# One 2048-column split instruction per weight chunk and engine in place of two of 1024 columns

## The chip, the cores and the metric

The kernel runs on one core of a Trainium2 chip. The metric is the device time of one execution in microseconds (us), taken as the median of several runs. A profiled execution of the same program gives the trace; times inside it count from the start of its span.

## The reference

One inference step of a two-layer decoder trunk, all in float32: 256 prompt tokens and 64 sample tokens (320 together), model width 1024. Each layer adds a token mixer to the residual and then a channel mixer, both after an RMS norm. The mixer is one wide projection, a chunked spatial gate, a gated linear recurrence, two branch projections and an output projection. The channel mixer is a dense SwiGLU in layer 0, and in layer 1 a top-2-of-8 mixture of SwiGLU experts, cut to

```python
h = h + mix
hn = rms_norm(h, norm_ffn_g[l])
# layer 0
h = h + (silu(hn @ w_gate) * (hn @ w_up)) @ w_down
# layer 1
for e in range(8):
    h = h + combine[..., e:e+1] * swiglu(hn, w_gate[e], w_up[e], w_down[e])
```

The weights are most of the data: eight experts of three 1024 x 2816 matrices each.

## The kernel before, in words

Each product of float32 matrices is made from three matmuls in a faster format: a weight w is split into a high part (w rounded) and a low part (w minus the high part), the moving data likewise, and high x high, high x low and low x high are summed in PSUM.

All weights stream through one ring in the order in which they are used. The unit is a chunk of 2048 columns on 128 partitions (1 MB). A chunk is made of two pieces of 1024 columns; `RING` is six pieces, so three chunks (`AHEAD` is 3). There are three rings of the same shape: `raw` (float32 from HBM), `whi` (high) and `wlo` (low). For piece p these steps follow each other:

- SyncE (the SP queue) waits until `low_done` counts p - 6 + 1, then loads the piece into its slot of `raw` (L495 in the dense layers, L503 in the experts).
- ScalarE (ACT) waits for the load and, through `pe_mark`, until TensorE (PE) has used piece p - 6, then copies `raw` to `whi` (`split_high` at L638, `high_of` at L850), and counts `high_done`.
- VectorE (DVE) waits for `high_done` and writes `raw` minus `whi` to `wlo` (`split_low` at L920, `low_of` at L1273), and counts `low_done`.
- PE waits for `low_done` and multiplies: L1413 to L1415 (dense), L1429 to L1431 (products by rows of tokens), L1694 to L1696 (expert down), L1703 to L1705 (expert gate and up).

ACT and DVE run one list each, chunk by chunk. In the entry of chunk c they split the two pieces of chunk c + 3. Between these two splits stands the work that empties the tiles of chunk c out of PSUM: activations of gates and of q, u, v on ACT (L664, L864), products, residual additions and squares (L954, L649, L931, L1287). Behind the second split stands the rest of the entry: the recurrence, the layer norm of v, the scores, and in the experts the turning of hidden rows. Because an engine works its list in order, a split that waits for PE holds back what is written after it.

In the dense layers a chunk is 48 matmuls of 320 columns. Between stages stand the RMS norms: PE is done with the last chunk, DVE adds the residual, ACT squares, DVE sums, PE reduces over partitions (L1438), ACT takes the root (L655), PE spreads it (L1446), and the next products follow.

An expert is 33 chunks of 12 matmuls of 512 columns (or 24 of 256): 11 of gate, 11 of up in turn, then 11 of down. PE takes the routed tokens of the next expert together (`gather`, L1657) after the last up chunk, number 21, and adds an expert's result back three chunks into the next expert (`scatter`, L1734). DVE then adds the six parts to the sum (`add_sums`, L1316), in its list between the splits of chunks 5 and 6 of that next expert; PE's gate products of the second group wait for the first of these additions.

Of the kernel before, what the change touches and what calls it, by code (L numbers as in the profile page):

```python
# [5 lines left out]
def hybrid_trunk_program(nc, A, OUT):  # L6
# [15 lines left out]
    F = mybir.dt.float32  # L22
# [599 lines left out]
    def _(act):  # L622
# [8 lines left out]

        def split_high(c, half):
            n = piece_width(c)
            p = 2 * c + half
            act.wait_ge(raw_full[p % RING], 16 * (p // RING + 1))
            if p >= RING:
                act.wait_ge(pe_mark, mark_after[p - RING])
            fn(whi[:, p % RING, 0:n], raw[:, p % RING, 0:n], ACT.Copy).then_inc(high_done, 1)  # L638

# [28 lines left out]
        for j in range(KD):  # L668
            square(0, j)
        split_high(0, 0)  # L670
        split_high(0, 1)
        norm(0)
        for c in range(1, AHEAD):
            split_high(c, 0)
            split_high(c, 1)

# [5 lines left out]
        for L in range(LAYERS):  # L682
            if L:
                norm(2 * L)
            for i, (sec, part) in enumerate(MIX):
                c = base(L) + i
                split_high(c + AHEAD, 0)
                if SAMPLE_AT < i <= SAMPLE_AT + H:
# [49 lines left out]
                if sec == "w_out":  # L738
                    for j in (2 * part, 2 * part + 1):
                        square(2 * L + 1, j)  # L740
                split_high(c + AHEAD, 1)
                if i == GATES_AT:
# [48 lines left out]
            if L % 2 == 0:  # L791
                norm(2 * L + 1)

                act.wait_ge(pstate_out, 16 * (L + 1))
                act.wait_ge(vrow_out, 16 * (L + 1))
                for q in s0_out:
                    act.wait_ge(q, 16 * (L + 1))
                for i, (sec, part) in enumerate(FFN):
                    c = first_chunk[(L, "gate")] + i
                    split_high(c + AHEAD, 0)  # L800
                    if sec == "gate":
                        if part:
                            act.wait_ge(dve_emptied, tile[(L, "up", 2 * part - 1)][3])
                        for j in (0, 1):
                            empties(L, sec, 2 * part + j, sg[:, j, :], ACT.Silu)
                    if sec == "down" and part % 3 == 2:
                        for j in (0, 1):
                            square(2 * L + 2, 2 * (part // 3) + j)
                    split_high(c + AHEAD, 1)
# [34 lines left out]

        def high_of(item, i, half):
            n = piece_width(NDENSE + i % NEC)
            p = 2 * i + half
            act.wait_ge(raw_full[p % RING], 16 * (2 * NEC // RING) * item + 16 * (2 * NDENSE // RING + p // RING + 1))
            act.wait_ge(pe_mark, 2 * NEC * item + (MB + p - RING + 1))
            fn(whi[:, p % RING, 0:n], raw[:, p % RING, 0:n], ACT.Copy).then_inc(high_done, 1)  # L850

        def chunk(item, i, last, ahead):

            if i + AHEAD < last:
                high_of(item, i + AHEAD, 0)
            if i >= NEC:
# [3 lines left out]
            if kind == "gate" and closed:  # L860
# [3 lines left out]
                fn(sge[:, j % 2, 0:cols], bank[2 * (j % 2)][:, 0:cols], ACT.Silu).then_inc(gate_emptied, 1)  # L864
            if i + AHEAD < last:
                high_of(item, i + AHEAD, 1)
            if kind == "up" and closed:
# [16 lines left out]
        def extra(item, n):  # L884
            for i in range(AHEAD):
                for half in range(2):
                    high_of(item, i, half)
            expert_in_high(item)
            for i in range(NEC):
                chunk(item, i, NEC, False)  # L890
# [15 lines left out]
    def _(dve):  # L906
# [8 lines left out]

        def split_low(c, half):
            n = piece_width(c)
            p = 2 * c + half
            dve.wait_ge(high_done, p + 1)
            v.tensor_tensor(wlo[:, p % RING, 0:n], raw[:, p % RING, 0:n],  # L920
                            whi[:, p % RING, 0:n].bitcast(F), ALU.subtract).then_inc(low_done, 1)

# [41 lines left out]
        add_square(0, KD - 1)  # L964
        split_low(0, 0)
        split_low(0, 1)
        dve.wait_ge(prm_ready, 1)

        v.tensor_tensor(lbt[:, 0], prm[:, P_LB + H:P_LB + 2 * H], prm[:, P_LB:P_LB + H], ALU.subtract).then_inc(lb_ready, 1)
        norm(0)  # L970
        for c in range(1, AHEAD):
            split_low(c, 0)
            split_low(c, 1)
        dve.wait_ge(lb_exp, 1)
# [6 lines left out]
        for L in range(LAYERS):  # L981
# [12 lines left out]
            for i, (sec, part) in enumerate(MIX):  # L994
                c = base(L) + i
                split_low(c + AHEAD, 0)
                if sec == "branch_a":
# [89 lines left out]
                split_low(c + AHEAD, 1)  # L1087
                if i == 0:
# [100 lines left out]
            if L % 2 == 0:  # L1189
                norm(2 * L + 1)  # L1190
                for i, (sec, part) in enumerate(FFN):
                    c = first_chunk[(L, "gate")] + i
                    split_low(c + AHEAD, 0)
                    if sec == "up":
# [11 lines left out]
                    split_low(c + AHEAD, 1)  # L1206
                    if sec == "up":
# [60 lines left out]

        def low_of(item, i, half):
            n = piece_width(NDENSE + i % NEC)  # L1270
            p = 2 * i + half
            dve.wait_ge(high_done, 2 * NEC * item + (2 * NDENSE + p + 1))
            v.tensor_tensor(wlo[:, p % RING, 0:n], raw[:, p % RING, 0:n],  # L1273
                            whi[:, p % RING, 0:n].bitcast(F), ALU.subtract).then_inc(low_done, 1)

        def chunk(item, i, last, ahead, e=None):

            if i + AHEAD < last:
                low_of(item, i + AHEAD, 0)
            if i >= NEC:  # L1280
# [3 lines left out]
            if kind == "up" and closed:  # L1284
# [3 lines left out]
                                ALU.mult).then_inc(he_ready, 1)  # L1288
            if i + AHEAD < last:
                low_of(item, i + AHEAD, 1)  # L1290
            if kind == "up" and closed:
# [57 lines left out]
        with dve.If(any_extra(dve)):  # L1349

            with dve.Fori(1, BLOCKS) as b:
                dve.wait_ge(pick_ready, NE)
                dve.wait_ge(shift_done, b)
                v.tensor_scalar(slot[:], slot[:], -float(CAP), None, ALU.add).then_inc(shift_done, 1)
                with dve.Fori(0, NE) as e:
                    more, item = extra_block(dve, b * NE + e - NE)
                    with dve.If(more):
                        choose(item, e, b + 1)
                        for i in range(AHEAD):
                            for half in range(2):  # L1360
                                low_of(item, i, half)
# [419 lines left out]
```

## Time and profile before

| | us |
|---|---|
| median of 3 runs | 1717.65 (1717.3 to 1717.74) |
| span of the profiled execution | 1711.7 |
| PE busy in it | 1651.6 |
| DVE busy | 1218.1 |
| ACT busy | 992.3 |

The span is the time from the first to the last instruction of the profiled execution; the median of the runs lies 5.95 us above it. Busy time is the sum over the whole span. The experts take the stretch from 860 to 1690 us; the dense stages lie before it. A chain of work, as the page gives it, is followed back from the last instruction to what released each step; a wait is the idle time of an engine, put down to what ended it.

### The profile page before, as it was taken

Reading aid. Unit: us, or ns where it says so; the run is one execution under the profiler, and the core shown is the slowest. Engines: PE = TensorE matmul, PEld = TensorE weight load, DVE = VectorE, ACT = ScalarE, POOL = GpSimd, SP = SyncE. Lnnn points to the kernel's source line nnn. Section 1 sums busy time; section 2 is a strip of 40 time slices with the busy share of each in tenths; the row PEclk is TensorE's granted clock in tenths of the full one; section 3 lists DMA queues with packets and bytes.
Section 4 is the critical chain, followed back from the end, with each engine's and each line's share of the span. In section 5 each row is a group of like instructions: output and inputs, shape, how many; then the busy total and the mean of one; then the engine's idle time right before and its main releaser. Section 6 shows DMA issues by size and latency. Waiting matters only on the chain.

```text
span 1711.7 us, 26087 instructions
## 1 busy us (share of the span) xinstructions
PE 1651.6 (96%) x9174; PEld 1450.4 (85%) x9175; DVE 1218.1 (71%) x1521; ACT 992.3 (58%) x1179; POOL 70.9 (4%) x87
## 2 busy tenths in 40 slices
PE   6989999999998989999899999999999999999996
PEld 5889999999998879999788888888888888888884
DVE  6677347544445487437478997979979799797996
ACT  5663234444334754224376786767867677776783
POOL 3020110000000020110000000000000000000000
PEclk9999999999998999989899999999999999999998
DMA  7434445355444334444278998989989899898994
GB/s 218 136 102 134 137 141 144 115 149 151 140 151 123 111 111 127 142 136 124 62 261 306 336 377 291 347 290 340 379 289 347 291 340 376 294 347 289 342 365 152
DMA packets 219374, 385.73 MB, mean 225 GB/s; under 512 B 11936, under 2 KB 103120, under 8 KB 219296
## 3 DMA queue, kind: packets, MB, share of 16 engines
q1 hardware_dynamic: 215920, 372.84, 63.8%
q0 software_dynamic: 3376, 11.83, 2.5%
q8 instruction: 51, 0.84, 0.2%
q14 instruction: 27, 0.22, 0.0%
HBM read 378.33 MB, written 6.29 MB: 225 GB/s over the span
## 4 chain that ended last, share of the span: by engine, by line
PE 90%; DVE 4%; ACT 4%; issue 2%; DMA 0%; SPq 0%; DVEq 0%; ACTq 0%
PE bank L1413 11%; PE bank L1415 10%; PE bank L1414 10%; PE bank L1703 9%; PE bank L1705 9%; PE bank L1704 9%; PE bank L1694 5%; PE bank L1695 5%; PE bank L1696 5%; PE bank L1657 4%; PE bank L1538 2%; ACT weights_high L638 1%; PE bank L1668 1%; PE bank L1588 1%; PE bank L1583 1%
## 5 line engine op out<-in xcount | busy, mean ns | idle before, releaser
L1273 DVE TENSOR_TENSOR weights_low<-weights_raw,weights_high 128x1024 fp32r<-128x1024 f32 x522 | 624.6, 1221 | 60.7 <-ACT weights_high L850 54.2
L850 ACT ACTIVATE weights_high<-weights_raw 128x1024 fp32r<-128x1024 f32 x522 | 548.6, 1061 | 158.9 <-PE bank L1705 63.5
L920 DVE TENSOR_TENSOR weights_low<-weights_raw,weights_high 128x1024 fp32r<-128x1024 f32 (+1 forms) x186 | 225.3, 1216 | 299.9 <-ACT weights_high L638 299.8
L638 ACT ACTIVATE weights_high<-weights_raw 128x1024 fp32r<-128x1024 f32 (+1 forms) x186 | 193.5, 1045 | 250.6 <-PE bank L1415 241.1
L1413 PE MATMUL bank<-moving_high,weights_high 128*128 128x320 f32 x992 | 318.2, 321 | 6.3 <-DVE moving_low L944 5.3
L1414 PE MATMUL bank<-moving_low,weights_high 128*128 128x320 f32 x992 | 313.5, 316 | 0.0
L1415 PE MATMUL bank<-moving_high,weights_low 128*128 128x320 f32 x992 | 313.2, 316 | 0.0
L1703 PE MATMUL bank<-weights_high,expert_in_high 128*128 128x512 f32 (+1 forms) x768 | 289.2, 377 | 0.0
L1705 PE MATMUL bank<-weights_high,expert_in_low 128*128 128x512 f32 (+1 forms) x768 | 286.2, 373 | 0.0
L1704 PE MATMUL bank<-weights_low,expert_in_high 128*128 128x512 f32 (+1 forms) x768 | 286.0, 372 | 0.0
L1413 PEld LDWEIGHTS bank<-moving_high,weights_high 128*128 128x128 f32 x992 | 192.7, 194 | 11.9 <-issue 8.3
L1414 PEld LDWEIGHTS bank<-moving_low,weights_high 128*128 128x128 f32 x992 | 192.9, 194 | 0.0
L1415 PEld LDWEIGHTS bank<-moving_high,weights_low 128*128 128x128 f32 x992 | 192.5, 194 | 0.0
L1705 PEld LDWEIGHTS bank<-weights_high,expert_in_low 128*128 128x128 f32 x768 | 145.0, 189 | 25.6
L1703 PEld LDWEIGHTS bank<-weights_high,expert_in_high 128*128 128x128 f32 x768 | 145.2, 189 | 25.0 <-issue 0.2
L1704 PEld LDWEIGHTS bank<-weights_low,expert_in_high 128*128 128x128 f32 x768 | 145.3, 189 | 24.4
L1694 PE MATMUL bank<-weights_high,expert_hidden_high 128*128 128x512 f32 x352 | 140.3, 398 | 0.0
L1695 PE MATMUL bank<-weights_low,expert_hidden_high 128*128 128x512 f32 x352 | 139.5, 396 | 0.0
L1696 PE MATMUL bank<-weights_high,expert_hidden_low 128*128 128x512 f32 x352 | 139.5, 396 | 0.0
L1696 PEld LDWEIGHTS bank<-weights_high,expert_hidden_low 128*128 128x128 f32 x352 | 66.3, 188 | 16.1
L1694 PEld LDWEIGHTS bank<-weights_high,expert_hidden_high 128*128 128x128 f32 x352 | 66.3, 188 | 15.8
L1695 PEld LDWEIGHTS bank<-weights_low,expert_hidden_high 128*128 128x128 f32 x352 | 66.3, 188 | 15.8
(283 smaller groups left out, 1880.3 us busy)
## 6 DMA issues: line engine op xcount, KB each, us to landing
weights_raw<-in_moe_w_gate SPq DMA_DIRECT2D x176, 512.0 KB, 5.5
weights_raw<-in_moe_w_up SPq DMA_DIRECT2D x176, 512.0 KB, 5.4
weights_raw<-in_moe_w_down SPq DMA_DIRECT2D x176, 512.0 KB, 5.2
weights_raw<-in_w_in SPq DMA_DIRECT2D x80, 512.0 KB, 3.5
weights_raw<-in_dense_w_gate SPq DMA_DIRECT2D x22, 512.0 KB, 3.8
weights_raw<-in_dense_w_up SPq DMA_DIRECT2D x22, 512.0 KB, 3.8
weights_raw<-in_w_out SPq DMA_DIRECT2D x16, 512.0 KB, 3.4
weights_raw<-in_dense_w_down SPq DMA_DIRECT2D x16, 512.0 KB, 3.4
```

The lines of the kernel that those rows point to most:

```text
L850: fn(whi[:, p % RING, 0:n], raw[:, p % RING, 0:n], ACT.Copy).then_inc(high_done, 1)
L920: v.tensor_tensor(wlo[:, p % RING, 0:n], raw[:, p % RING, 0:n], whi[:, p % RING, 0:n].bitcast(F), ALU.subtract).then_inc(low_done, 1)
L1273: v.tensor_tensor(wlo[:, p % RING, 0:n], raw[:, p % RING, 0:n], whi[:, p % RING, 0:n].bitcast(F), ALU.subtract).then_inc(low_done, 1)
L1413: mm(b[:, 0:T], whi[:, p % RING, w], mh[:, k0 + k, :], start=first and k == 0, stop=False)
L1414: mm(b[:, 0:T], whi[:, p % RING, w], ml[:, k0 + k, :], start=False, stop=False)
L1415: ins = mm(b[:, 0:T], wlo[:, p % RING, w], mh[:, k0 + k, :], start=False, stop=last and ends)
L1694: mm(bank[down_bank(ahead) + hh][:], heh[:, kk, :], whi[:, p % RING, w], start=kk == 0, stop=False)
L1695: mm(bank[down_bank(ahead) + hh][:], heh[:, kk, :], wlo[:, p % RING, w], start=False, stop=False)
L1696: ins = mm(bank[down_bank(ahead) + hh][:], hel[:, kk, :], whi[:, p % RING, w], start=False, stop=kk == KF - 1)
L1703: mm(b[:, 0:cols], xeh[:, kk, :], whi[:, p % RING, w], start=kk == 0, stop=False)
L1704: mm(b[:, 0:cols], xeh[:, kk, :], wlo[:, p % RING, w], start=False, stop=False)
L1705: ins = mm(b[:, 0:cols], xel[:, kk, :], whi[:, p % RING, w], start=False, stop=kk == KD - 1)
```

## The change

Each engine splits a chunk with one instruction over both pieces of the ring (2 x 1024 columns side by side) where it had one for each piece. ACT waits for both loads and until PE has used both pieces of the old chunk; `high_done` and `low_done` then rise by two at once. DVE waits until both pieces are high. The split takes the place of the first of the two old splits in each engine's list; the second one is gone. The loads, the ring and PE's list are as before, so a load still waits for the same count of `low_done`.

```diff
-        def split_high(c, half):
+        def split_high(c):
             n = piece_width(c)
-            p = 2 * c + half
-            act.wait_ge(raw_full[p % RING], 16 * (p // RING + 1))
+            p = 2 * c
+            s = p % RING
+            act.wait_ge(raw_full[s], 16 * (p // RING + 1))
+            act.wait_ge(raw_full[s + 1], 16 * (p // RING + 1))
             if p >= RING:
-                act.wait_ge(pe_mark, mark_after[p - RING])
-            fn(whi[:, p % RING, 0:n], raw[:, p % RING, 0:n], ACT.Copy).then_inc(high_done, 1)
+                act.wait_ge(pe_mark, mark_after[p + 1 - RING])
+            fn(whi[:, s:s + 2, 0:n], raw[:, s:s + 2, 0:n], ACT.Copy).then_inc(high_done, 2)
...
-                split_high(c + AHEAD, 0)
+                split_high(c + AHEAD)
...
-                split_high(c + AHEAD, 1)
...
-        def high_of(item, i, half):
+        def high_of(item, i):
...
-            act.wait_ge(pe_mark, 2 * NEC * item + (MB + p - RING + 1))
-            fn(whi[:, p % RING, 0:n], raw[:, p % RING, 0:n], ACT.Copy).then_inc(high_done, 1)
+            act.wait_ge(raw_full[s], landed)
+            act.wait_ge(raw_full[s + 1], landed)
+            act.wait_ge(pe_mark, 2 * NEC * item + (MB + p - RING + 2))
+            fn(whi[:, s:s + 2, 0:n], raw[:, s:s + 2, 0:n], ACT.Copy).then_inc(high_done, 2)
...
-        def split_low(c, half):
+        def split_low(c):
             n = piece_width(c)
-            p = 2 * c + half
-            dve.wait_ge(high_done, p + 1)
-            v.tensor_tensor(wlo[:, p % RING, 0:n], raw[:, p % RING, 0:n],
-                            whi[:, p % RING, 0:n].bitcast(F), ALU.subtract).then_inc(low_done, 1)
+            p = 2 * c
+            s = p % RING
+            dve.wait_ge(high_done, p + 2)
+            v.tensor_tensor(wlo[:, s:s + 2, 0:n], raw[:, s:s + 2, 0:n],
+                            whi[:, s:s + 2, 0:n].bitcast(F), ALU.subtract).then_inc(low_done, 2)
...
-            if i + AHEAD < last:
-                low_of(item, i + AHEAD, 1)
```

`low_of` in the experts changes as `split_low` does, and the calls in the channel mixer and in the rarely taken extra blocks likewise.

## Rows read from the trace of the kernel before

**Rows 1.** The page: busy time by engine, and the ending chain by engine.

```profile
PE 1651.6 (96%) x9174; PEld 1450.4 (85%) x9175; DVE 1218.1 (71%) x1521; ACT 992.3 (58%) x1179; POOL 70.9 (4%) x87
...
PE 90%; DVE 4%; ACT 4%; issue 2%; DMA 0%; SPq 0%; DVEq 0%; ACTq 0%
```

**Rows 2.** The ending chain in order of time: start, us, what; two gathers, transposes.

```profile
1029.26 8.26 PE bank L1657 x48
1093.78 0.59 PE bank L1668 x4
1134.58 8.26 PE bank L1657 x48
```

**Rows 3.** Busy time by engine in one expert's period, clock, DMA share, GB/s.

```profile
1150.70:1256.00 105.30, 105.30 (x506) 86.71 (x506) 91.93 (x94) 76.97 (x84) 0.00 (x0) 1.00 0.91 329
```

**Rows 4.** Waits of PE's weight loads, 860 to 1690 us: total, times, longest.

```profile
PEld bank L1711 <- issue: 1.3, 8, 0.2
```

**Rows 5.** Timeline of ACT in the down products: start, us, operation, idle before.

```profile
1046.36 1.06 ACT L850 ACTIVATE weights_high<-weights_raw 128x1024 fp32r<-128x1024 f32 x1 [0.35 <-PE bank L1696]
1047.76 1.06 ACT L850 ACTIVATE weights_high<-weights_raw 128x1024 fp32r<-128x1024 f32 x1 [0.34 <-PE bank L1696]
```

**Rows 6.** Waits of ACT, 860 to 1690 us: for the raw weights.

```profile
ACT weights_high L850 <- DMA weights_raw<-in_moe_w_up: 16.2, 40, 1.1
```

**Rows 7.** Groups by line and shape: count, busy us, mean ns, idle before.

```profile
L1273 DVE TENSOR_TENSOR weights_low<-weights_raw,weights_high 128x1024 fp32r<-128x1024 f32 x522 | 624.6, 1221 | 60.7 <-ACT weights_high L850 54.2
L850 ACT ACTIVATE weights_high<-weights_raw 128x1024 fp32r<-128x1024 f32 x522 | 548.6, 1061 | 158.9 <-PE bank L1705 63.5 <-PE bank L1696 55.6 <-DMA weights_raw<-in_moe_w_up 16.2
L1316 DVE SCALAR_TENSOR_TENSOR sum_rows<-bank,gate_now,sum_rows 128x512 f32<-128x512 f32 x32 | 21.8, 746 | 1.7 <-PE bank L1735 0.8
L1053 DVE TENSOR_TENSOR query_decayed<-query,level_decay 128x1280 f32<-128x1280 f32 x2 | 3.0, 1492 | 0.1
L751 ACT ACTIVATE level_product<-level_product 128x1280 f32<-128x1280 f32 x2 | 2.5, 1273 | 0.0
```

**Rows 8.** The ending chain in the first mixer, at q.

```profile
57.50 1.04 ACT weights_high L638
...
59.86 0.45 ACT query L664
...
60.35 0.44 PE bank L1429
```

**Rows 9.** Landing of one load, issued alone at 1041.8 (L503).

```profile
DMA to landing us min/median/max: 3.6/3.6/3.6
```

**Rows 10.** Landing of two loads (L503): first issued at 802.9, second below.

```profile
L503 SPq DMA_DIRECT2D weights_raw<-in_moe_w_up x1: 373/373/373, 803.5 to 803.5; - x1
...
DMA to landing us min/median/max: 3.6/3.9/4.3
```

**Rows 11.** Landing in the stream: 1084.9 and 1086.7; then 1043.2 to 1062.

```profile
DMA to landing us min/median/max: 3.6/4.0/4.4
...
DMA to landing us min/median/max: 4.8/5.2/5.5
```

**Rows 12.** Timeline at the norm after 298 us.

```profile
298.51 0.47 ACT L649 ACTIVATE squares<-residual 128x320 f32<-128x320 f32 x1 [0.76 <-DVE residual L954]
298.89 1.04 ACT L638 ACTIVATE weights_high<-weights_raw 128x1024 fp32r<-128x1024 f32 x1
...
301.77 1.07 PE L1446 MATMUL bank<-identity,inverse_rms 128*128 128x128 f32 x6 [1.38 <-DVE inverse_rms L936]
```

**Rows 13.** The ending chain in the first mixer, at v and the scores.

```profile
93.85 1.06 ACT weights_high L638
...
115.46 3.61 PE bank L1538 x16
```

**Rows 14.** PE in two stretches: us, busy, granted clock, DMA share, GB/s.

```profile
304.60:310.86 6.26, 6.26 (x26) 0.57 0.00 0
...
843.70:858.70 15.00, 14.96 (x48) 0.50 0.01 2
```

More of the change, by code:

```diff
@@ L669, in _ @@
             square(0, j)
-        split_high(0, 0)
-        split_high(0, 1)
+        split_high(0)
         norm(0)
         for c in range(1, AHEAD):
-            split_high(c, 0)
-            split_high(c, 1)
+            split_high(c)
         act.wait_ge(lb_ready, 1)
@@ L799, in _ @@
                     c = first_chunk[(L, "gate")] + i
-                    split_high(c + AHEAD, 0)
+                    split_high(c + AHEAD)
                     if sec == "gate":
@@ L808, in _ @@
                             square(2 * L + 2, 2 * (part // 3) + j)
-                    split_high(c + AHEAD, 1)
                     if sec == "up":
@@ L843, in hidden_high @@
             fn(heh[:, ts[0]:ts[-1] + 1, :], bank[4 + j % 2][:, 0:128 * len(ts)], ACT.Copy).then_inc(heh_ready, 1)
-        def high_of(item, i, half):
+        def high_of(item, i):
             n = piece_width(NDENSE + i % NEC)
-            p = 2 * i + half
-            act.wait_ge(raw_full[p % RING], 16 * (2 * NEC // RING) * item + 16 * (2 * NDENSE // RING + p // RING + 1))
-            act.wait_ge(pe_mark, 2 * NEC * item + (MB + p - RING + 1))
-            fn(whi[:, p % RING, 0:n], raw[:, p % RING, 0:n], ACT.Copy).then_inc(high_done, 1)
+            p = 2 * i
+            s = p % RING
+            landed = 16 * (2 * NEC // RING) * item + 16 * (2 * NDENSE // RING + p // RING + 1)
+            act.wait_ge(raw_full[s], landed)
+            act.wait_ge(raw_full[s + 1], landed)
+            act.wait_ge(pe_mark, 2 * NEC * item + (MB + p - RING + 2))
+            fn(whi[:, s:s + 2, 0:n], raw[:, s:s + 2, 0:n], ACT.Copy).then_inc(high_done, 2)
         def chunk(item, i, last, ahead):
             if i + AHEAD < last:
-                high_of(item, i + AHEAD, 0)
+                high_of(item, i + AHEAD)
             if i >= NEC:
@@ L864, in chunk @@
                 fn(sge[:, j % 2, 0:cols], bank[2 * (j % 2)][:, 0:cols], ACT.Silu).then_inc(gate_emptied, 1)
-            if i + AHEAD < last:
-                high_of(item, i + AHEAD, 1)
             if kind == "up" and closed:
@@ L885, in extra @@
             for i in range(AHEAD):
-                for half in range(2):
-                    high_of(item, i, half)
+                high_of(item, i)
             expert_in_high(item)
@@ L914, in link @@
             dve.wait_ge(dve_link, links[0])
-        def split_low(c, half):
+        def split_low(c):
             n = piece_width(c)
-            p = 2 * c + half
-            dve.wait_ge(high_done, p + 1)
-            v.tensor_tensor(wlo[:, p % RING, 0:n], raw[:, p % RING, 0:n],
-                            whi[:, p % RING, 0:n].bitcast(F), ALU.subtract).then_inc(low_done, 1)
+            p = 2 * c
+            s = p % RING
+            dve.wait_ge(high_done, p + 2)
+            v.tensor_tensor(wlo[:, s:s + 2, 0:n], raw[:, s:s + 2, 0:n],
+                            whi[:, s:s + 2, 0:n].bitcast(F), ALU.subtract).then_inc(low_done, 2)
         def add_square(n, j):
@@ L964, in _ @@
         add_square(0, KD - 1)
-        split_low(0, 0)
-        split_low(0, 1)
+        split_low(0)
         dve.wait_ge(prm_ready, 1)
@@ L971, in _ @@
         for c in range(1, AHEAD):
-            split_low(c, 0)
-            split_low(c, 1)
+            split_low(c)
         dve.wait_ge(lb_exp, 1)
@@ L995, in _ @@
                 c = base(L) + i
-                split_low(c + AHEAD, 0)
+                split_low(c + AHEAD)
                 if sec == "branch_a":
@@ L1086, in _ @@
                         add_square(2 * L + 1, j)
-                split_low(c + AHEAD, 1)
                 if i == 0:
@@ L1192, in _ @@
                     c = first_chunk[(L, "gate")] + i
-                    split_low(c + AHEAD, 0)
+                    split_low(c + AHEAD)
                     if sec == "up":
@@ L1205, in _ @@
                             add_square(2 * L + 2, 2 * (part // 3) + j)
-                    split_low(c + AHEAD, 1)
                     if sec == "up":
@@ L1267, in hidden_low, with low_of @@
                             ALU.subtract).then_inc(hel_ready, 1)
-        def low_of(item, i, half):
+        def low_of(item, i):
             n = piece_width(NDENSE + i % NEC)
[L1271 to L1274, printed above, removed]
+            p = 2 * i
+            s = p % RING
+            dve.wait_ge(high_done, 2 * NEC * item + (2 * NDENSE + p + 2))
+            v.tensor_tensor(wlo[:, s:s + 2, 0:n], raw[:, s:s + 2, 0:n],
+                            whi[:, s:s + 2, 0:n].bitcast(F), ALU.subtract).then_inc(low_done, 2)
         def chunk(item, i, last, ahead, e=None):
             if i + AHEAD < last:
-                low_of(item, i + AHEAD, 0)
+                low_of(item, i + AHEAD)
             if i >= NEC:
@@ L1288, in chunk @@
                                 ALU.mult).then_inc(he_ready, 1)
-            if i + AHEAD < last:
-                low_of(item, i + AHEAD, 1)
             if kind == "up" and closed:
@@ L1359, in _ @@
                         for i in range(AHEAD):
-                            for half in range(2):
-                                low_of(item, i, half)
+                            low_of(item, i)
                         expert_in_low(item)
```

## The prediction

> **What bounds the kernel now.** I read the page first: TensorE is busy 96% of the 1711.7 us span and nearly alone on the chain that ended last [rows 1]. An average over stages says little, so I read the expert stretch next (860 to 1690 us, half of the span). Between two gathers of routed tokens lie 105.3 us [rows 2], and TensorE (PE) is busy for every one of them while VectorE (DVE) is busy 91.9 and ScalarE (ACT) 77.0 [rows 3]; PE's weight loads wait 1.3 us in 830 [rows 4], for nothing that the splits do. So PE sets the pace there and the splitting of weights runs ahead of it. How far ahead is the question, since the change makes the splits coarser. In the down products ACT starts a half chunk's high part every 1.40 us and is idle 0.34 or 0.35 us before each until PE releases it [rows 5]: PE takes 2.8 us per chunk, and a half chunk of the ring of three chunks is split the moment PE has let go of it. ACT also waits for the raw weights themselves, 40 times for "up" alone, never above 1.1 us [rows 6]: the raw ring is hardly early now.
>
> **The cost of one split.** A 1024-column high part takes 1.061 us; ACT's 1280-column activation takes 1.273, which is 0.83 ns per column more. For 2048 columns that gives H = 1.061 + 1024 x 0.00083 = 1.91 us (2.12 if it were two of the old ones). DVE's subtraction takes 1.221 us at 1024 and 1.492 at 1280 columns, so L = 1.221 + 1024 x 0.00106 = 2.31 us (bound 2.44) [rows 7]. Per chunk ACT saves 0.21 us and DVE 0.13, on engines for which PE does not wait in the experts: worth nothing there by itself.
>
> **What the change moves.** Three things become later. (1) A high part may start only when PE has finished the whole old chunk in its slots, not half of it. (2) The low part starts after both halves are high. (3) low_done rises by two at the end of the long subtraction, so the SP queue can issue the two loads of the chunk three further on only then, where it issued one load per half, some 1.4 us apart.
>
> The PE side of the ring stands this: PE ends chunk c, H + L + handovers = 1.91 + 2.31 + 0.2 = 4.4 us later chunk c+3 is ready, and PE still has 5.6 us of c+1 and c+2. The raw side does not. One lap of a raw slot is X = P + H + L + handovers, where P is the time from the first issue of a pair to the landing of its second half. Three handovers (DVE to SP, DMA to ACT, ACT to DVE) I put at 0.3 us, an estimate: a bank that ACT frees is taken up by PE 0.04 us later in [rows 8], and the issue costs more. X = P + 4.5, and PE needs one lap every 3 x 2.8 = 8.4 us. The lap holds if P is under 3.9 us.
>
> P is not in the trace as such. A single half chunk issued alone lands in 3.6 us [rows 9]. Two issued half a microsecond apart could land by 0.5 + 3.6 = 4.1 us if the second were not slowed at all. The nearest case, two issued some 0.6 us apart (802.9 and 803.5) on an idle queue, had the second landing 0.6 + 4.3 = 4.9 us after the first issue [rows 10]. Two issued 1.8 us apart in the running stream took 1.8 + 4.4 = 6.2 us, and single halves in the full stream take 4.8 to 5.5, median 5.2 [rows 11]. I take P = 5.2: above the idle pair's 4.9 because the previous chunk's pair will still be landing. Ends: 4.1 and 6.1. So X = 9.7 us (8.6 to 10.6), and the lap is 1.3 us too long: PE will wait for weights_low.
>
> The Trainium skill's page "DMA: Bandwidth & Descriptors" (section "Latency and other measured facts") says a DMA's fixed cost shrinks as HBM is loaded less. The trace agrees in direction, with 3.6 us alone against a median of 5.2 in the stream. By that rule P would fall back to 4.9 as the stream slows, and the experts would cost 22 us less than below.
>
> **Sum for one expert period**, by the ring's own steps, chunks numbered 0 to 32, L(c) the end of a chunk's low part. The gather stands between chunks 21 and 22: PE ends 21 at L(21) + 2.8, spends 8.3 us on the gather and 0.6 on transposes before it, some 0.2 after it [rows 2], then 22 and 23 (5.6); 26 is split 4.3 us later: L(26) = L(21) + 21.8. From 26 the raw laps rule: 26, 29, 32, and of the next expert 2, 5: four laps. DVE then runs the six additions of the previous expert's sums (0.746 us each [rows 7], with a copy 4.8 us), which in its order stand between the low parts of 5 and 6, so L(6) = L(5) + 4.8 + 2.3. From 6 five more laps lead to 21. Period = 21.8 + 7.1 + 9 X = 28.9 + 9 X: with 9.7 it is 116.2 us against 105.3, +10.9; with X = 8.6 it is 106.3 (+1.0); with 10.6, 124.3 (+19.0). Without the head start that the raw loads get during the gather it would be eleven laps of excess. Eight experts (the first has no laps before 6, the last none of the gather's relief, which about cancel): **+87 us**, bounds +8 and +152.
>
> **Dense stages.** There a chunk is 48 matmuls of 320 columns against 12 of 512, 2.5 times the columns, so some 7 us at the same pace, and neither side of the ring is late; what costs is order. In three norms (one after each mixer, one after the dense channel mixer) the chain is last residual, square, DVE's sum, root, spread. In before the last square runs at 298.51, the second half's high part stands behind it, at 298.89, and the spread starts at 301.77 [rows 12]. After the change ACT's full H and DVE's full L come ahead of residual and square, since both wait for the same PE mark: 1.9 + 2.3 + small, with the table load then covered, +4.2 us each: 13 us for three. If DVE's split is still hidden by the table load, 3 each. In each layer's mixer the chain runs through ACT: a half split at 57.50, a table load (58.54 to 59.86, 1.3 us), then the activation of q that frees PE's bank [rows 8]. A whole split in place of a half adds 0.85 us there and 0.85 in the entry before, and in that entry a table load and an activation (1.3 + 0.45), which ran before PE ended its chunk, now come behind the split: +3.5. Later the chain goes ACT half, DVE half, level products, the layer norm of v, a DVE half again, and ends in PE at 115.46 [rows 13]; whole splits at two steps add (1.91 + 2.31) - (1.06 + 1.22) = 1.9 each, +3.9; the high parts of the gated branch, needed soon after, +1. That is 8.4 per layer, 17 for two, and 1 at the start. **+31 us**, bounds 18 (three at each norm, half of the mixers' hidden) and 45 (layer 1's longer forget chain costs double).
>
> Total by the profiled execution: 1711.7 + 87 + 31 = 1829.7; the median of the runs lies 5.95 us above the span (1717.65 - 1711.7), so **1836 us**. Bounds: 1718 + 8 + 18 = 1744 and 1718 + 152 + 45 = 1915.
>
> **Rivals.** (a) Mild: P near 4.1, because two transfers issued together overlap. For it: each alone is 3.6. Against it: the idle pair's 4.9. Then only the dense part and a few microseconds are left: 1745 to 1795.
> (b) The clock: PE's gaps let its clock fall from 2.4 GHz to 1.2. For it: after an idle stretch at the norm the granted clock was 0.57 for the first 6.26 us of the next chunk, and in the first gather 0.50 for 15.0 us, 6.7 us more than the same gather later [rows 2, 14]. A fall costs about 6.26 x 0.43 = 2.7 us. Once per lap, PE's lap would be 8.4 + 2.7 = 11.1, 1.4 over X: 9 x 8 x 1.4 = 101 more, 1937. Against it: the gaps would be some 1.3 us long between full bursts.
> (c) Faster, by the saved fixed cost: ACT 0.21 and DVE 0.13 us per chunk reach the end where both halves of a split stand on the chain, at most some twenty places in the dense stages, 20 x 0.34 = 7 us: 1711. It decides if P is under 3.9 us and the old half-early start was idle lead; [rows 6] and [rows 12] speak against both. The Trainium skill's "Perfetto Trace Analysis" (section "Optimizing Scalar/DVE Operations") has both sides: larger operations help a saturated engine, smaller ones help where the engine causes bubbles elsewhere. DVE at 91.9 of 105.3 us is not saturated here.
> (d) No change: the splits stay ahead everywhere: 1718. As (c), and the norms' order hidden too.
>
> **How the numbers follow.** Forecast (raw laps too long, 1795 to 1915) 0.75, (a) 0.11, (b) 0.07, (c) 0.04, (d) 0.03. About 0.2% (3.4 us) is what a measurement of this kernel can tell from no change. The range 1744 to 1915 is the bounds and leaves out (b), (c) and (d), 0.14. Faster 0.04, same 0.03, slower 0.93.
>
> **What would show it.** In the profile after: high parts of 1.91 and low parts of 2.31 us; SP issues in pairs, the second landing about 5 us after the first issue; in the experts PE waiting for DVE's weights_low, ACT's longest wait being the DMA of weights_raw and no longer PE; gathers 116 us apart; moved data near 300 GB/s there instead of 329 [rows 3]; the gaps at the norms 4 us longer. If PE does not wait in the experts, P was too high and (a) holds; if its clock there is below 1.00, (b).

## The result, and the profile after the change

The changed kernel takes 1929.08 us (median; 1922.28 to 1934.12) where the kernel before, run beside it, takes 1717.47 us: a ratio of 1.124 with a 95% interval of 1.120 to 1.127. The prediction was 1836 us, with a range of 1744 to 1915. The direction was right, and the time lies 14 us above the range.

The page of the changed kernel, to be read against [rows 1] and [rows 7]: busy time by engine; the ending chain by engine; then the two groups of splits in the experts (count, busy us, mean ns of one, idle time before them and what ended it).

```profile
PE 1715.5 (89%) x9174; PEld 1459.4 (76%) x9175; DVE 1178.3 (61%) x1167; ACT 931.2 (48%) x825; POOL 71.9 (4%) x87
...
PE 47%; DVE 16%; DMA 15%; ACT 11%; issue 8%; SPq 2%; DVEq 0%; ACTq 0%
...
L1269 DVE TENSOR_TENSOR weights_low<-weights_raw,weights_high 128x2048 fp32r<-128x2048 f32 x261 | 596.9, 2289 | 225.5 <-ACT weights_high L851 225.3
L851 ACT ACTIVATE weights_high<-weights_raw 128x2048 fp32r<-128x2048 f32 x261 | 500.3, 1917 | 345.7 <-DMA weights_raw<-in_moe_w_gate 101.9
```

ACT and DVE are less busy than before, by 61 and 40 us: the longer instructions do save their fixed cost, and with 1.917 and 2.289 us they last what the prediction had worked out from [rows 7]. Yet PE, nearly alone on the chain before, now holds 47% of it. The rest went to DVE, DMA and ACT, one behind the other: that is a lap of the ring, load, high part, low part, load.

The span grew from 1711.7 to 1920.5 us. The first gather of routed tokens divides it. It starts at 935.88 us where it started at 843.75, so the dense part costs **92.1 us**; the rest of the span went from 868.0 to 984.6, so the experts cost **116.7 us**. The place of this division varies by some 5 us between executions of the same dense part: in five other kernels of this study whose dense part is that of the kernel before, the first gather starts between 844.2 and 848.4 us.

**The experts.** Two gathers of the changed kernel in the ending chain (start, us, what), against [rows 2]:

```profile
1146.95 8.26 PE bank L1650 x48
1266.70 8.26 PE bank L1650 x48
```

The same period as a stretch, against [rows 3]: length, then busy time and count of PE, PEld, DVE, ACT and POOL, granted clock, DMA share, GB/s.

```profile
1146.79:1266.54 119.75, 110.62 (x508) 85.22 (x506) 88.90 (x61) 70.80 (x50) 0.00 (x0) 1.00 0.86 289
```

A period is 119.75 us instead of 105.3, at a granted clock of 1.00; PE is idle for 9 us of it and moved data falls from 329 to 289 GB/s. What PE waits for in the experts is the low part of the weights (960 to 1900 us: total, times, longest):

```profile
PE bank L1696 <- DVE weights_low L1269: 34.9, 70, 1.6
```

A lap of one raw slot, from the ending chain in order of time:

```profile
1293.12 2.30 DVE weights_low L1269
...
1296.16 4.27 DMA weights_raw<-in_moe_w_down
...
1300.64 1.93 ACT weights_high L851
...
1302.66 2.30 DVE weights_low L1269
```

From the start of one low part to the start of the low part that works on the load it released, 9.54 us pass: 2.30 of DVE, 0.74 until the second load of the pair is issued, 4.27 until it has landed, 1.93 of ACT and 0.30 of handovers. PE needs such a lap every 8.4 us. Nothing in this chain is PE's: it waits for the ring.

**The dense part.** PE from 24 us to the first gather, before and then after (length, PE busy, granted clock, DMA share, GB/s):

```profile
24.00:843.75 819.75, 787.84 (x5098) 0.97 0.43 131
```

```profile
24.00:935.88 911.88, 808.42 (x5097) 0.94 0.37 118
```

The same matmuls keep PE busy 20.6 us longer, at a clock of 0.94 instead of 0.97, and the time in which PE does nothing grows from 31.9 to 103.5 us, by 71.6. What ended it: waits of PE in this part (us in total, times, longest), of the kernel before and then of the changed one.

```profile
PE bank L1538 <- DVE scores L1138: 10.6, 2, 5.7
...
PE bank L1438 <- DVE square_sum L931: 5.2, 3, 1.9
```

```profile
PE bank L1406 <- DVE weights_low L919: 24.0, 6, 4.9
PE bank L1431 <- DVE square_sum L930: 19.6, 3, 6.6
PE bank L1531 <- DVE scores L1134: 15.4, 2, 7.7
PE bank L1406 <- DVE b_low L984: 14.2, 4, 6.9
```

Square sums (the norms) and scores are places of the prediction, and so is the wait for the query (8.5 us in all, 1.4 before). Not among them are the waits for `b_low` and four of the six waits of the largest line, 19.7 of its 24.0 us (the other two stand in branch a). They stand in the stage that normalises the output of the recurrence into branch b, multiplies it and merges the branches. The kernel before there (timeline: start, us, engine, line, operation, idle before it and what ended that):

```profile
245.59 1.06 ACT L638 ACTIVATE weights_high<-weights_raw 128x1024 fp32r<-128x1024 f32 x1 [1.28 <-PE bank L1415]
246.67 1.22 DVE L920 TENSOR_TENSOR weights_low<-weights_raw,weights_high 128x1024 fp32r<-128x1024 f32 x1 [2.11 <-ACT weights_high L638]
247.82 0.48 DVE L1076 TENSOR_TENSOR query<-query,bank 128x320 f32<-128x320 f32 x1
```

And the changed kernel:

```profile
270.93 1.91 ACT L640 ACTIVATE weights_high<-weights_raw 128x2048 fp32r<-128x2048 f32 x1 [11.45 <-PE bank L1408]
272.94 2.29 DVE L919 TENSOR_TENSOR weights_low<-weights_raw,weights_high 128x2048 fp32r<-128x2048 f32 x1 [13.20 <-ACT weights_high L640]
275.15 0.48 DVE L1073 TENSOR_TENSOR query<-query,bank 128x320 f32<-128x320 f32 x1
```

Before, ACT's half was released in the middle of a chunk (PE runs it from 241.72 to 253.01), and DVE began on b at 247.82 while PE still multiplied. After, ACT sits idle for 11.45 us until PE has ended its chunk (270.81), then both whole splits run, and only then, at 275.15, does DVE begin on b. This work used to run beside PE's chunk, and PE waited for only 1.1 us from 240 to 272 us; now PE waits for it.

### The profile page after: what moved, and what is told of

Same layout as the page of the kernel before. It is cut to its first block, busy times and chain, and to the rows that moved or that the text cites. A ratio compares the mean times of both kernels' runs of the same rounds, so it can differ in the third digit from the quotient of the medians.

```text
span 1920.5 us, 25691 instructions
## 1 busy us (share of the span) xinstructions
PE 1715.5 (89%) x9174; PEld 1459.4 (76%) x9175; DVE 1178.3 (61%) x1167; ACT 931.2 (48%) x825; POOL 71.9 (4%) x87
## 4 chain that ended last, share of the span: by engine, by line
PE 47%; DVE 16%; DMA 15%; ACT 11%; issue 8%; SPq 2%; DVEq 0%; ACTq 0%
PE bank L1406 10%; PE bank L1407 10%; PE bank L1408 10%; DVE weights_low L1269 9%; ACT weights_high L851 7%; DMA weights_raw<-in_moe_w_up 7%; DMA weights_raw<-in_moe_w_down 5%; PE bank L1650 4%; DMA weights_raw<-in_moe_w_gate 3%; ACT weights_high L640 2%; SPq L503 1%; DVE weights_low L919 1%; PE bank L1531 1%; DVE expert_hidden L1283 1%; PE bank L1687 1%
## 5 line engine op out<-in xcount | busy, mean ns | idle before, releaser
L1269 DVE TENSOR_TENSOR weights_low<-weights_raw,weights_high 128x2048 fp32r<-128x2048 f32 x261 | 596.9, 2289 | 225.5 <-ACT weights_high L851 225.3
L851 ACT ACTIVATE weights_high<-weights_raw 128x2048 fp32r<-128x2048 f32 x261 | 500.3, 1917 | 345.7 <-DMA weights_raw<-in_moe_w_gate 101.9
L919 DVE TENSOR_TENSOR weights_low<-weights_raw,weights_high 128x2048 fp32r<-128x2048 f32 (+1 forms) x93 | 210.9, 2269 | 425.7 <-ACT weights_high L640 425.6
L1696 PE MATMUL bank<-weights_high,expert_in_high 128*128 128x512 f32 (+1 forms) x768 | 302.9, 394 | 52.5 <-DVE weights_low L1269 34.9
L640 ACT ACTIVATE weights_high<-weights_raw 128x2048 fp32r<-128x2048 f32 (+1 forms) x93 | 175.8, 1892 | 342.9 <-PE bank L1408 320.4
L1687 PE MATMUL bank<-weights_high,expert_hidden_high 128*128 128x512 f32 x352 | 144.2, 410 | 9.0 <-DVE weights_low L1269 8.4
```

Source lines behind the costliest of these rows:

```text
L640: fn(whi[:, s:s + 2, 0:n], raw[:, s:s + 2, 0:n], ACT.Copy).then_inc(high_done, 2)
L851: fn(whi[:, s:s + 2, 0:n], raw[:, s:s + 2, 0:n], ACT.Copy).then_inc(high_done, 2)
L919: v.tensor_tensor(wlo[:, s:s + 2, 0:n], raw[:, s:s + 2, 0:n], whi[:, s:s + 2, 0:n].bitcast(F), ALU.subtract).then_inc(low_done, 2)
L1269: v.tensor_tensor(wlo[:, s:s + 2, 0:n], raw[:, s:s + 2, 0:n], whi[:, s:s + 2, 0:n].bitcast(F), ALU.subtract).then_inc(low_done, 2)
L1687: mm(bank[down_bank(ahead) + hh][:], heh[:, kk, :], whi[:, p % RING, w], start=kk == 0, stop=False)
L1696: mm(b[:, 0:cols], xeh[:, kk, :], whi[:, p % RING, w], start=kk == 0, stop=False)
```

## The experiments

**The two parts apart.** Is the loss the sum of two, and is each what it seems? The first kernel splits whole chunks in the dense layers alone, the second in the experts alone.

`whole_high` and `whole_high_of` stand here and below for the changed kernel's `split_high(c)` and `high_of(item, i)`; DVE's lists are edited in the same way. In `dense_whole`, against the kernel before:

```diff
-                split_high(c + AHEAD, 0)
+                whole_high(c + AHEAD)
...
-                split_high(c + AHEAD, 1)
```

In `experts_whole`:

```diff
-                high_of(item, i + AHEAD, 0)
+                whole_high_of(item, i + AHEAD)
...
-                high_of(item, i + AHEAD, 1)
```

> The whole split in the two dense layers alone; the experts split by halves as in the kernel before. If the loss is the sum of two separate parts, the first gather comes at about 936 us as in the changed kernel (844 in the kernel before), the expert periods are 105.3 us again, and the time is about 1717 + 92 = 1809 us. Rival: the dense loss came about because something of the expert stretch reaches back (the shared ring, the clock); then the first gather would come before 900 us and the sum of the two separate kernels' losses would fall short of 200 us.

Measured: 1810.08 us, ratio 1.054 (1.051 to 1.058). Gathers in its ending chain, the first one and two later ones:

```profile
935.88 15.03 PE bank L1671 x48
...
1121.50 8.26 PE bank L1671 x48
1226.82 8.26 PE bank L1671 x48
```

> The whole split in the experts alone; the dense layers as before. Raw laps too long: first gather at about 844 us, periods of 119.5 us, the pair of loads landing 5.2 us after its first issue, PE waiting for weights_low; time 1717 + 117 = 1834 us. Rival (the expert loss is a late start of the ring handed over by the dense part): periods near 105 and a time under 1760 us.

Measured: 1838.72 us, ratio 1.071 (1.068 to 1.074). Gathers:

```profile
847.93 15.03 PE bank L1671 x48
...
1057.62 8.26 PE bank L1671 x48
1177.04 8.26 PE bank L1671 x48
```

The first gather of `dense_whole` stands at 935.88 as in the changed kernel, with periods of 105.3; `experts_whole` has 119.4. Their losses, 92.5 and 121.1 us, add up to 213.6, against 211.6 of the whole change. The two parts are separate, and each can be studied alone.

**Order or size, in the dense part.** The whole split differs from the two halves in three things: its length, its release by PE's whole chunk, and its place ahead of the rest of the entry. Two kernels pull these apart. `halves_front` keeps halves but puts both at the place of the first one, in the dense layers and in the experts; `dense_whole_late` keeps the whole split in the dense layers but puts it at the place of the second one.

```diff
                 split_high(c + AHEAD, 0)
+                split_high(c + AHEAD, 1)
...
-                split_high(c + AHEAD, 1)
```

> Both halves as two instructions per engine, but both at the place of the first split, in dense layers and experts. Order theory of the dense part (what costs is that a split that waits for PE's end of the chunk stands ahead of the entry's other work): the dense part loses most of what the changed kernel loses, 55 to 85 us, first gather at 899 to 929 us. Size theory (what costs is the 2048-column instruction and its coarse marks): the dense part loses under 15 us. For the experts the raw-lap theory says that a half's lap is a single landing of some 4.7 us + 1.06 + 1.22 + 0.35 = 7.3 us, under PE's 8.4, so periods of 105.3 to 106.5 us; if the place in the list were the cause there too, 115 or more. Time by order and laps: 1772 to 1812 us.

Measured: 1773.25 us, ratio 1.033 (1.030 to 1.036). Gathers:

```profile
907.81 15.03 PE bank L1655 x48
...
1092.22 8.26 PE bank L1655 x48
1197.54 8.26 PE bank L1655 x48
```

The first gather is 64.1 us late with no long instruction in the kernel: order alone makes two thirds of the 92. That is within the order theory's 55 to 85. The experts are at 105.3, so there the place costs nothing. PE up to that gather (length, busy, clock, DMA share, GB/s):

```profile
24.00:907.80 883.80, 815.27 (x5097) 0.93 0.40 121
```

Of the 64.1 us, 27.4 are longer matmuls at the lower clock and 36.6 are idle time, half of the 71.6 of the changed kernel. The other half of the idle time needs the whole split at that place; whether by its length or by its release was not separated.

```diff
-                split_high(c + AHEAD, 0)
...
-                split_high(c + AHEAD, 1)
+                whole_high(c + AHEAD)
```

> The whole split in the dense layers at the place of the second old split, behind the work that empties the chunk's tiles; experts by halves as before. Order theory: nearly all of the 92 us comes back except where work behind the second split (norm roots, branch b's normalising, scores) still stands behind it, so a loss of 0 to 30 us, 1717 to 1747 us. Size theory: the loss stays above 60 us, over 1777 us.

Measured: 1724.81 us, ratio 1.0047 (1.003 to 1.0064). Its first gather, and PE up to it (length, busy, clock, DMA share, GB/s):

```profile
855.89 15.03 PE bank L1671 x48
```

```profile
24.00:855.90 831.90, 787.72 (x5098) 0.97 0.40 129
```

Of 92.1 us, 80 are back, and PE's busy time is that of the kernel before: the clock's 20.6 us went with the gaps. The waits of PE between 240 and 282 us, the stage of branch b, hold no weights any more; the longest is 1.6:

```profile
PE bank L1427 <- DVE branch_product L1022: 1.8, 2, 1.6
```

Of the 12.3 us of idle time that are left, 8 are before the scores (15.0 us against 10.6) and at the norms (waits for the inverse root: 6.0 against 2.4), where work behind the second split still waits for it. So the next kernels move the split behind everything.

**The split behind all other work.** In each entry of a token mixer, at the norms behind the norm itself; `dense_whole_last` moves the whole split there, `dense_second_last` only the second half of the kernel before.

```diff
-                split_high(c + AHEAD, 1)
...
+                if i + 1 < len(MIX):
+                    split_high(c + AHEAD, 1)
             if L % 2 == 0:
                 norm(2 * L + 1)
+                split_high(base(L) + len(MIX) - 1 + AHEAD, 1)
```

> The whole split of a chunk in the dense layers (experts by halves), but behind all other work of its entry, at a norm behind the norm. Order theory: the 92 us of the dense part were the place, not the size of the instruction, so they all come back: 1708 to 1718 us. Size theory (a 2048-column instruction that needs PE's whole chunk is itself too coarse there): at least the 7 us of the late place remain, 1724 us or more.

Measured: 1714.43 us, ratio 0.9986 (0.9977 to 0.9996). All 92 us are back with 2048-column instructions: behind the other work, their size and their release by PE's whole chunk cost at most the 4.5 us by which the next kernel, with halves, is faster.

> Splits by halves everywhere, as in the kernel before, but in the dense layers the second half's split stands behind all other work of its entry on ScalarE and VectorE, at a norm behind the norm. If the order of the split against chain work is what costs, this gains where the kernel before still has a half split on the chain: 0.8 us at each of three norms (root waits for 1.04 us of high part) and 1.2 to 2.3 us before the scores of each layer, 5 to 7 us in all: 1710 to 1713 us. Rival: the later split makes the raw ring late in the dense part, or the chain's next step is late anyway: 1717 us or more.

Measured: 1709.96 us, ratio 0.9961 (0.9947 to 0.9974), the fastest kernel of this study. Its waits of PE in the dense part:

```profile
PE bank L1548 <- DVE scores L1143: 7.0, 2, 3.5
```

The waits for the scores fell from 10.6 to 7.0 us and the one for the decayed query rose from 1.5 to 2.7. At the norms only the wait for the inverse root fell, from 2.4 to 1.1 us, less than the 0.8 at each that was expected. PE's idle time up to the first gather fell by 6.0 us in all (31.9 to 25.9). The same order that cost the changed kernel 92 us still cost the kernel before some 6.

**What the experts' lap is made of.** All four kernels below leave the dense part as before and start from `experts_whole` (119.4 us a period). In the first, ACT's high part is made in two halves and DVE's low part stays whole.

```diff
-                whole_high_of(item, i + AHEAD)
+                high_of(item, i + AHEAD, 0)
+                high_of(item, i + AHEAD, 1)
```

> Experts alone: ScalarE makes the high part in two halves, both at the first place, each released by its own load and its own half of PE's old chunk; VectorE's low part stays whole. Raw-lap theory: the lap of a raw slot (last landing, high part, low part, next landing) shortens by 1.92 - 1.06 = 0.86 us, because the first half's high part runs while the second half lands: lap 9.9 to 9.05, and in some ten laps of a period 8.6 us: gathers 111 us apart (119.5 with both whole), about 1770 us. Rival (the whole low part and its double release of the loads is all that matters): period stays above 117.

Measured: 1770.1 us, ratio 1.032 (1.026 to 1.037). Two gathers:

```profile
1045.25 8.26 PE bank L1662 x48
1157.86 8.26 PE bank L1662 x48
```

This period is 112.6 us, and the six after the first are 111.6 on average against 111 expected: what is taken out of the lap comes back once per lap.

```diff
-                    sp.dma_start(raw[:, p % RING, 0:kt // 2 * cols].rearrange("p (k n) -> p k n", n=cols),
-                                 rows(A["moe_w_" + kind][0, e], k0 + half * (kt // 2), kt // 2, c0, cols)).then_inc(
+                    sp.dma_start(raw[:, p % RING, 0:kt // 2 * (cols // 2)].rearrange("p (k n) -> p k n", n=cols // 2),
+                                 rows(A["moe_w_" + kind][0, e], k0 + half * (kt // 2), kt // 2, c0, cols // 2)).then_inc(
```

> Experts alone with both parts whole, and each load brings only half of its columns (the other half of each piece is whatever the slot held: the output is not the reference's). Nothing else differs: same instructions, same waits. Raw-lap theory: the pair lands in 3.6 to 4.2 us instead of 5.2, the lap falls to 8.3 to 8.9 us, at or near PE's 8.4, and the period to 105.3 to 110 us, about 1718 to 1760. Rival (the two long instructions and the marks of PE are the cause, not the landing): 119.5 us as before.

Measured: 1733.17 us, ratio 1.009 (1.007 to 1.012). The landing of a load (issue to landing) and two gathers:

```profile
DMA to landing us min/median/max: 2.4/2.9/3.3
```

```profile
1038.10 8.26 PE bank L1671 x48
1144.55 8.26 PE bank L1671 x48
```

With both long instructions and both coarse releases in place, only the landing shorter (median 2.9 us against 4.3), the period falls to 106.45. The pair is there 3.5 us after its first issue (median), under the 3.9 that the prediction gave as the limit, and a period is 1.1 us too long instead of 14. So it is the lap of the raw ring that costs, and the rival that needs only the instructions and PE's marks falls.

```diff
-                for half in range(2):
...
-                    sp.wait_ge(low_done, 2 * NEC * item + (2 * NDENSE + p - RING + 1))
...
+                sp.wait_ge(low_done, 2 * NEC * item + (2 * NDENSE + p - RING + 2))
+                sp.dma_start(raw[:, s:s + 2, :].rearrange("p h (k n) -> p (h k) n", n=cols),
+                             rows(A["moe_w_" + kind][0, e], k0, kt, c0, cols)).then_inc(raw_full[s], 16)
```

> Experts alone with both parts whole; a chunk is loaded by one DMA of 1 MB on one semaphore instead of two of 512 KB. It takes the second issue, 0.55 us after the first, out of the lap. If the second landing is late because it is issued later, the lap falls by up to 0.5 us and the period to 114.5 to 117 us; if it is late because of its bytes (1 MB at some 360 GB/s takes 2.9 us whichever way it is cut), the period stays at 118.5 to 120.5 us.

Measured: 1824.36 us, ratio 1.063 (1.058 to 1.068). Its landing, and two gathers:

```profile
DMA to landing us min/median/max: 4.8/5.1/6.5
```

```profile
1170.32 8.26 PE bank L1668 x48
1288.83 8.26 PE bank L1668 x48
```

The period is 118.5 us: one load of 1 MB lands in 5.1 us, hardly before the pair does, and about 1 us is gained. The second issue is a small part of the landing; the bytes are the large one.

```diff
-                whole_low_of(item, i + AHEAD)
+                low_of(item, i + AHEAD, 0)
+                low_of(item, i + AHEAD, 1)
```

> Experts alone: ScalarE's high part whole, VectorE's low part in two halves, which release the two loads one after the other. Raw-lap theory: the low part takes 2.44 us in all, but the first load starts 1.22 us earlier and only the second load's own landing, some 4.5 us, stands in the lap: 0.1 + 4.5 + 1.92 + 2.44 + 0.3 = 9.3 us against 9.9, so periods of 113 to 116 us and about 1800 us. Rival (the coarse release of the loads is the whole cause): back to 105 to 107 us. Other rival (the release does not matter, DMA has a fixed pace): 119 or more.

Measured: 1825.38 us, ratio 1.064 (1.057 to 1.071), a miss: some 25 us above the 1800 expected. Two things in its trace bear on it. The lap shortened less than expected: taken from the end of a chunk's low part to that of the chunk three further on, its median over 258 laps is 9.73 us, against 10.06 in `experts_whole` and 9.3 expected. And the clock fell. PE in three stretches (length, busy, clock, DMA share, GB/s), then the wait of PE that falls in the first of them:

```profile
1116.00:1119.00 3.00, 0.52 (x3) 1.00 0.88 287
1119.00:1122.00 3.00, 2.25 (x6) 0.71 0.94 320
1122.00:1125.00 3.00, 3.00 (x11) 0.73 0.29 113
```

```profile
PE bank L1710 <- DVE sum_rows L1323: 3.2, 1, 3.2
```

PE waits 3.2 us for the first of DVE's six additions, and the granted clock in the 6 us after that is 0.71 and 0.73. Such a gap of over 3 us stands in each of seven experts, two of the gathers take 14.0 and 14.2 us instead of 8.26 (behind waits of 1.9 and 1.8 us), and from 900 to 1700 us the mean clock is 0.96 where `experts_whole` has 1.00. The periods are 117.4 to 125.1 us, 120.1 on average, where 113 to 116 were expected and `experts_whole` has 119.4: up to the last gather nothing is gained, and the gain of some 10 us lies behind it. How much of the miss is the clock's and how much the lap's was not separated.

## Why the prediction was right and wrong

**The direction and the mechanism in the experts were right.** H and L are 1.92 and 2.29 us (1.91 and 2.31 in the sum). The pair lands 5.2 us after its first issue (median of the expert chunks; 5.2 taken). Gathers are 119.75 us apart where 116.2 was said. Most of ACT's waits for a high part now end with the DMA (241 of 341 us from 960 to 1900 us), and PE waits for weights_low. The clock is 1.00 in the period, so rival (b) has no part there, and that the measured 1929 us lies near its 1937 is chance; rivals (a), (c) and (d) fall with P and with the time. The first segment of the sum and the others, from five low parts of one period (ends are start plus duration):

```profile
1139.54 2.29 DVE L1269 TENSOR_TENSOR weights_low<-weights_raw,weights_high 128x2048 fp32r<-128x2048 f32 x1 [0.69 <-ACT weights_high L851]
...
1163.31 2.29 DVE L1269 TENSOR_TENSOR weights_low<-weights_raw,weights_high 128x2048 fp32r<-128x2048 f32 x1 [0.52 <-ACT weights_high L851]
...
1202.62 2.29 DVE L1269 TENSOR_TENSOR weights_low<-weights_raw,weights_high 128x2048 fp32r<-128x2048 f32 x1 [1.08 <-ACT weights_high L851]
...
1209.07 2.27 DVE L1269 TENSOR_TENSOR weights_low<-weights_raw,weights_high 128x2048 fp32r<-128x2048 f32 x1
...
1259.05 2.29 DVE L1269 TENSOR_TENSOR weights_low<-weights_raw,weights_high 128x2048 fp32r<-128x2048 f32 x1 [0.84 <-ACT weights_high L851]
```

| step | predicted | measured |
|---|---|---|
| L(21) to L(26), over the gather | 21.8 | 23.8 |
| four laps to L(5) | 38.8 | 39.3 |
| L(5) to L(6), the additions | 7.1 | 6.4 |
| five laps to L(21) | 48.5 | 50.0 |
| period | 116.2 | 119.5 |

The laps are 9.9 us on average instead of 9.7: the three handovers, put at 0.3 us, take 0.46 in the lap shown above (0.16 of it before the first of the two issues). The first segment is 2 us longer because PE reaches the gather at 1146.8, 1.6 us after the time that L(21) + 2.8 + 0.6 gives; 0.7 of that is a wait for DVE's product of the hidden rows, which now stands behind a whole low part. Eight times 3.3 us are 26 of the 30 by which +87 fell short of +116.7, still inside that term's bounds of +8 to +152.

The prediction held against this a rule of the Trainium skill, "DMA: Bandwidth & Descriptors", section "Latency and other measured facts", by which a transfer's fixed cost shrinks under lighter load. A single half does land sooner than before (median 4.3 us against 5.3 between 1000 and 1600 us), in agreement with it; the pair's landing, which makes the lap, did not fall to the 4.9 us that would have followed.

**The step that failed is the sum of the dense part**: +31 us, with bounds 18 and 45, and measured +92.1. By places, from the starts of the same matmuls before and after, layer 0 and layer 1:

| place | predicted | measured |
|---|---|---|
| start | 1 | 0.2 |
| three norms | 13 | 5.7, 4.6, 7.2: 17.5 |
| q chain | 3.5 each | 5.1, 5.0 |
| v, u and scores | 3.9 each | 5.3, 4.7 |
| gated branch a | 1 each | 4.5, 4.7 |
| normalising of b, branch b, merge | nothing | 25.1, 25.1 |
| output gate, gate b | nothing | -1.6, -3.1 |

One stage is missing from it, and that stage alone costs 50 us; without it the measured loss would be 42, inside the sum's bounds. The prediction took its steps from the chain that ended last, but passed over this stretch, in which PE hardly waits. The chain does leave PE there (kernel before, start, us, what):

```profile
245.59 1.06 ACT weights_high L638
...
249.78 0.49 DVE b_low L987
...
254.46 0.45 ACT gate_b L664
```

It goes from PE's mark in the middle of a chunk (245.5) through ACT's half split and DVE's and ACT's work on b, beside PE's multiplying, and comes back to PE at 254.95. PE's waits were short, but the work had no slack left: released at the end of PE's chunk, it came out into the open. The text named this order as what costs in the dense part, and applied it only to the norms, to q, to v and the scores, and with 1 us to branch a, which cost 4.5. `halves_front`, with 64 of the 92 us and no long instruction, shows that the order does two thirds of it; `dense_whole_late` and `dense_whole_last` show that behind the other work the size costs next to nothing.

A second thing was left out of that sum. Rival (b), the clock, was weighed for the experts alone. It hardly came there (from 960 to 1860 us it fell once, for 6.8 us, at a wait of 2.9 us); it came in the dense part, where the gaps are long: 20.6 of the 92.1 us are the same matmuls at a clock of 0.94 (the places of the table contain them).

Of the 93 us by which the median lies above the forecast, 61 are the dense part, 30 the experts, and 2.6 the distance between the profiled execution and the median, put at 5.95 and here 8.6: it is no fixed cost.

**Rival (c)** said that the fixed cost saved could show as a gain. No run shows that: `dense_whole_last` is 0.14% faster than the kernel before, but it has another order too, and `dense_second_last`, which moves second halves alone and keeps the small instructions, gains more (0.39%). The Trainium skill's "Perfetto Trace Analysis", section "Optimizing Scalar/DVE Operations", advises larger operations for a saturated engine and smaller ones where an engine that is not saturated causes bubbles elsewhere. The runs agree: DVE, at 91.9 of 105.3 us, had nothing to gain from larger operations, and cutting ACT's high part in two took 69 us off `experts_whole`.

## What to carry to other kernels

Before two instructions are merged, count the lap of the ring that they belong to (release, issue, landing of the last byte, each engine's whole instruction) against the time that the consumer takes for the ring's depth; a lap just under it has no room for a coarser step. Then list all work that stands behind the merged instruction in its engine's order, work that runs beside the consumer and makes it wait for next to nothing included: a short wait does not say that there is slack, and a release that comes at the end of the consumer's chunk instead of its middle turns such work into waiting. An instruction that only prepares something for three chunks later belongs behind everything that somebody waits for now.

## What the runs showed of the hardware

Cutting a 1 MB load into two or one made little difference to when its last byte was there: 5.1 us for one load, 5.2 from the first issue of a pair to its last landing, in a stream that moved some 290 GB/s; half the bytes per load, in a stream of 162 GB/s, landed in 2.9 us instead of 4.3.

PE's granted clock was 1.00 in an expert period of the changed kernel with waits of up to 1.3 us for weights and one of 2.3 us for the additions. In `experts_dve_halves`, where that one wait was 3.2 us, the clock over the 6 us behind it was 0.71 and 0.73, though PE was idle for less of that whole period (7.1 us against 9.1). The length of the wait alone does not decide it: in `experts_whole_one_load` that wait was 2.1 to 2.7 us in seven experts, and behind five of the seven the granted clock fell to 0.50 (behind one of 2.14 us, for example), while behind the other two (2.15 and 2.22 us) it stayed at 1.00.
